# Compressed scores by stationaries of 32 key columns and four transposes; the two low-rank up projections alternate

## The reference

```
dist_c = t[:, None] - cmp_end[None, :]
lc = einsum('bghqd,bgcd->bghqc', qb, kc_blk) + shared_bias(dist_c)
pc = masked_softmax(lc, dist_c >= 0)
```

```
w_log = -softplus(-(w0 + tanh(wd) @ w_up)) - 0.5
a = sigmoid(a0 + ad @ a_up)
```

## Time and profile before

| | us |
|---|---|
| median of 3 runs | 652.71 (652.45 to 653.73) |
| the profiled execution's own time | 653.95 |
| its span, first to last instruction | 652.2 |
| TensorE matmul busy | 601.5 (92%) |
| TensorE weight load busy | 440.4 (68%) |
| VectorE busy | 218.5 (33%) |
| ScalarE busy | 138.3 (21%) |
| GpSimd busy | 20.6 (3%) |
| mean granted TensorE clock | 0.974 |
| DMA | 158.94 MB, mean 244 GB/s |

### The profile page before, as it was taken

How to read it: one execution, slowest core, us unless ns; L and a number is a source line. 1 busy time by engine, 2 the same in 40 slices (tenths; PEclk the granted TensorE clock), 3 DMA queues, 4 the chain that set the end, 5 groups by cost and what they waited for, 6 DMA issues and landing times.

```text
span 652.2 us, 11747 instructions
## 1 busy us (share of the span) xinstructions
PE 601.5 (92%) x4948; PEld 440.4 (68%) x4948; DVE 218.5 (33%) x599; ACT 138.3 (21%) x352; POOL 20.6 (3%) x24
## 2 busy tenths in 40 slices
PE   8999999999999999999999999998989988757684
PEld 8988887888877877777788888894344442313331
DVE  3152448634343666356410222235121111102022
ACT  3010233032234363343411000001210111000013
POOL 1000000000300003001000000000000000000000
PEclk9999999999999999999999999998999999959797
DMA  8585344731211111101329994887999999999992
GB/s 318 194 319 180 113 151 158 297 130 66 70 62 67 66 66 66 66 4 66 124 94 423 419 396 155 349 359 270 416 420 421 420 421 420 422 421 421 422 388 107
DMA packets 27287, 158.94 MB, mean 244 GB/s; under 512 B 2896, under 2 KB 7136, under 8 KB 9440
## 3 DMA queue, kind: packets, MB, share of 16 engines
q1 hardware_dynamic: 24224, 137.71, 54.0%
q10 hardware_dynamic: 3008, 20.45, 7.5%
HBM read 157.07 MB, written 1.07 MB: 243 GB/s over the span
## 4 chain that ended last, share of the span: by engine, by line
PE 61%; issue 32%; DVE 3%; DMA 2%; ACT 1%; SPq 0%; POOL 0%; POOLq 0%; DVEq 0%; ACTq 0%
PE bank L612 42%; PE bank L843 3%; PE bank L946 2%; PE bank L644 2%; PE bank L975 2%; DMA ring<-front 1%; PE bank L995 1%; PE bank L627 1%; PE bank L959 1%; ACT tok L1589 1%; PE bank L880 1%; PE bank L1011 1%; PE bank L899 1%; PE bank L910 1%; PE bank L1061 0%
## 5 line engine op out<-in xcount | busy, mean ns | idle before, releaser
L612 PE MATMUL bank<-hT,ring 128*128 128x256 f32 x864 | 199.7, 383 | 0.6 <-issue 0.3
L612 PEld LDWEIGHTS bank<-hT,ring 128*128 128x128 f32 x864 | 159.6, 190 | 30.7 <-issue 10.4
L612 PE MATMUL bank<-yT,ring 128*128 128x256 f32 x256 | 55.4, 379 | 0.0
L612 PEld LDWEIGHTS bank<-yT,ring 128*128 128x128 f32 x256 | 48.6, 190 | 6.6
L1423 ACT ACTIVATE work<-bank 128x512 f32<-128x512 f32 (+2 forms) x44 | 22.6, 514 | 107.5 <-PE bank L1242 48.9
L1788 DVE TENSOR_TENSOR work<-bank,table 128x512 f32<-128x512 f32 (+1 forms) x22 | 11.6, 544 | 95.9 <-PE bank L1235 88.1
L1288 PE MATMUL bank<-ring,work 128*32 128x512 f32 (+1 forms) x192 | 33.8, 634 | 10.2 <-DMA yT<-experts 7.1
L1235 PEld LDWEIGHTS bank<-work,tok 128*128 128x128 f32 x256 | 31.0, 196 | 10.4 <-issue 10.4
L1589 ACT ACTIVATE tok<-tok,small 128x128 f32<-128x128 f32 (+1 forms) x64 | 28.5, 445 | 23.2 <-DVE small L2015 21.6
L1235 PE MATMUL bank<-work,tok 128*128 128x128 f32 x256 | 32.5, 282 | 0.8 <-DVE work L1792 0.8
L1226 PE MATMUL bank<-ring,work 128*32 128x512 f32 x240 | 30.0, 606 | 2.3 <-DMA ring<-experts 2.3
(11 more groups left out here) (257 smaller groups left out, 742.6 us busy)
## 6 DMA issues: line engine op xcount, KB each, us to landing
ring<-front SPq DMA_DIRECT2D x47, 1024.0 KB, 5.0
ring<-experts SPq DMA_DIRECT2D x40, 1024.0 KB, 25.4
work<-experts SPq DMA_DIRECT2D x9, 1024.0 KB, 27.6
ring<-experts ACTq DMA_DIRECT2D x8, 1024.0 KB, 12.6
table<-experts SPq DMA_DIRECT2D x6, 1024.0 KB, 27.4
yT<-experts SPq DMA_DIRECT2D x6, 1024.0 KB, 26.8
hT<-experts SPq DMA_DIRECT2D x4, 1024.0 KB, 24.6
work<-experts ACTq DMA_DIRECT2D x3, 1024.0 KB, 27.9
```

The source lines that it names most:

```text
L612: return first(pe.matmul(o, l, r, start=(k == 0), stop=(k == n - 1)))
```

## The change

The scores. `kcb` is laid out as group, copy, key, with 16 places for the 15 keys, so that the 32 columns of one group (two copies of 16) are one stationary matrix. One memset of the whole replaces the two, and the two copies out of PSUM write with a stride. For each of the eight pairs of heads one matmul moves all 256 tokens; four pairs go into the four quarters of 32 partitions of one bank, in two column halves. The result has keys along the partitions, so ScalarE copies the bank `cs` into SBUF (`csT`), and after the step "turn" TensorE waits for that copy and transposes it by four transposes into bank 3. VectorE reads both tiles' scores from there.

The up projections. `wup` and `aup` are issued alternately, matmul by matmul, for n = 0 and then n = 1. The order of use of the banks and ScalarE's order are as before.

```diff
-        kcb = dead[:, at:at + 2 * NG * NCMP].rearrange("p (q n) -> p q n", q=2)
+        kcb = dead[:, at:at + NG * 32].rearrange("p (g q n) -> p g q n", g=NG, q=2)
+        csT = xf[:, 1024:1536].rearrange("p (b t) -> p b t", b=2)
...
-        hand("cs0", 2), hand("cs1", 3)
+        hand("cs", 2)
...
+            if name == "kw":
+                hand("csT", 3)
...
             for n in range(2):
-                o = begin(f"wup{n}")
+                up = [(f"wup{n}", 0, begin(f"wup{n}")), (f"aup{n}", 32, begin(f"aup{n}"))]
                 for m in range(2):
                     c = (2 * n + m) * P
-                    last = pe.matmul(o[:, m * S:(m + 1) * S], pr("lora_up")[0:32, c:c + P], mix[0:32, 12, :],
-                                     start=True, stop=True)
-                end(last, f"wup{n}")
-            for n in range(2):
-                o = begin(f"aup{n}")
...
+                    for name, row, o in up:
+                        last = pe.matmul(o[:, m * S:(m + 1) * S], pr("lora_up")[row:row + 32, c:c + P], mix[row:row + 32, 12, :],
+                                         start=True, stop=True)
+                        if m:
+                            end(last, name)
...
-            for i in range(NT):
-                nc_ = 7 if i == 0 else NCMP
-                o = begin(f"cs{i}")
-                for m in range(8):
-                    g = m // 2
-                    last = pe.matmul(o[:, 2 * m * nc_:2 * (m + 1) * nc_], qT[:, m, i * P:(i + 1) * P],
-                                     kcb[:, :, g * NCMP:g * NCMP + nc_], start=True, stop=True)
-                end(last, f"cs{i}")
+            o = begin("cs")
+            for b in range(2):
+                for m in range(4):
+                    last = pe.matmul(o[32 * m:32 * m + 32, b * S:(b + 1) * S], kcb[:, 2 * b + m // 2, :, :].rearrange("p q n -> p (q n)"),
+                                     qT[:, 4 * b + m, :], start=True, stop=True)
+            end(last, "cs")
 
             early(RWKV_STEPS[0])
             late(RWKV_STEPS[0])
+            pe.wait_ge(q["cmp_kv_ready"], 2)
+            turned("csT", [csT[:, b, i * P:(i + 1) * P] for i in range(NT) for b in range(2)])
             project("kw", C_KW)
...
-            act.wait_ge(q["keys_zeroed"], 2)
+            act.wait_ge(q["keys_zeroed"], 1)
             for p in range(2):
-                ins = copy(kcb[64 * p:64 * p + 64, p, :], b0[64 * p:64 * p + 64, 0:60])
+                ins = copy(kcb[64 * p:64 * p + 64, :, p, 0:NCMP],
+                           b0[64 * p:64 * p + 64, 0:NG * NCMP].rearrange("p (g n) -> p g n", g=NG))
             give(ins, "cmp_kv_ready", "kcb")
             keys(0, "ks")
+            b0 = full(act, "cs")
+            give(copy(csT, flat(b0)), "cmp_kv_ready", "cs")
...
-            for p in range(2):
-                chain(dve.memset(kcb[64 * (1 - p):64 * (1 - p) + 64, p, :], 0.0), "keys_zeroed", hold=False)
+            chain(dve.memset(kcb, 0.0), "keys_zeroed", hold=False)
...
-                b0 = full(dve, f"cs{i}")
+                b0 = full(dve, "csT")
...
-                chain(tt(cp, b0[:, 0:NH * nc_].rearrange("p (h n) -> p h n", h=NH), back, ALU.add))
-                dve.sem_inc(bank_free[plan[f"cs{i}"][0]], 1)
+                scored = b0[:, i * S:(i + 1) * S].rearrange("p (h n) -> p h n", h=NH)[:, :, 0:nc_]
+                chain(tt(cp, scored, back, ALU.add))
+                if i == NT - 1:
+                    dve.sem_inc(bank_free[plan["csT"][0]], 1)
```

## The result

The changed kernel takes 647.95 us (median of 4 runs, 647.42 to 648.79) against 652.97 us of the kernel before timed beside it: 5.0 us less, ratio 0.992, 95% interval 0.9901 to 0.9939. Forecast were 649.2 us with a range from 648.3 to 651.7. Timed once more the kernel had 648.4 us against 652.63, ratio 0.9931 (0.9912 to 0.9951), 4.2 us. Over all timed executions of the two kernels, 13 of this kernel and 62 of the kernel before, the medians are 648.2 and 653.0 us, 4.8 us apart.

The account below looks back on a forecast made before the run. TensorE's instruction stream bounds the kernel to about 440 us, the weights' arrival after 455 us. Savings of 0.55 + 3.0 = 3.5 us took the median from 652.71 to 649.2 us, range 648.3 to 651.7.

Parts of the forecast that it names:

- Part A: Up projections: alternating wup and aup makes two row groups run side by side, saving 0.55 us, between nothing and 1.0.
- The wait for bank 0: Before kc: ScalarE frees the bank only at 76.81, so kc starts at about 77.0 instead of 76.53.
- both waits for banks absent: Lower end of the range, 648.3 us: neither kc nor the first transposes wait for a bank's reader.
- Part B: Scores and transposes: scores in 1.15 us, twenty transposes at full clock, kw at 144.4 instead of 147.45, saving 3.0 us.
- the wait for bank 5: Before tok00: VectorE frees the bank after bonus1, so transposes start at 141.9 instead of 141.56, costing 0.35 us.
- The experts' stage: The stage bound by the weights' DMA, full share from 455 us: same length, 3.5 us earlier.
- The cover on VectorE: Softmax before the first mask: VectorE is done at 150.9, the mask is due at 152.6, leaving 1.7 us.
- What reaches the end: TensorE's saving counts in full: DMA share before 455 us is only 0.48, so the DMA-bound stretch begins earlier.
- 1: Rival: clock falls in the transposes or at kw's start, as long as before; 650.7 to 650.9 us, chance 0.14.
- 4: Rival: clock falls at the first transpose and stays down in kw; slower, up to 657.6 us, chance 0.04.
- (3): Rival: the scores' column quarters do not overlap, 651.8 us, or VectorE is late, similar end; chance together 0.06.
- (2): Rival: the gain does not reach the end, the last 200 us of weights not hanging on TensorE; 652.5 us, chance 0.06.

Follow-up runs that it names:

- the kernel with other banks: The kernel after with kc in bank 7, bonus1 in bank 1 and the first atok in bank 4: 648.26 us, ratio 0.9923 to the kernel before.

## Why the prediction was wrong

What it says of TensorE's own time, of the waits for banks and of the side-by-side work held, in place and in nearly every size. What failed is how it took the granted clock: it read the clock of one execution, and put the same clock into every execution, before and after.

- Part A, TensorE's own time: forecast 0.55, measured 0.61 in every profile that has the new order and the wait (2.28 us against 2.89). The wait for bank 0 was there (0.28), as forecast; taking it away saved 0.36.
- Part A, the clock: this is the first place where the step failed. The prediction counted the clock behind the up projections as 1.00 because it was 1.00 in the profile of before, and so gave the new order no gain from it and the low end of the range no room. In 2 of 6 profiles with the old order `kc` runs at 1.2 GHz, 1.7 us; with the new one in none of 10. On the mean that is 0.6 us, as much as part A's whole forecast, if the counts are the true chances. The range's lower end, "both waits for banks absent", should have had the 1.7 in it.
- Part B: forecast 3.0, measured 3.25 in the first pair of profiles: twenty transposes 0.115 each and not 0.125, and the wait for bank 5, 0.22 of idle time, was worth 0.34 when taken away, against 0.35. The scores with both changes of the tile size took 1.21 us from the `bonus` stream's end where no wait stood behind them (the kernel with other banks, 141.34 - 138.42 - 1.71), against 1.15. But the term is a mean of two cases: 3.25 where the old scores brought the clock down (3 of 5), 1.66 where they did not (7.16 against 5.50). The prediction had only the first case, as certain. The mean is 2.6, so here the error went the other way, 0.4 us too much.
- The experts' stage: the prediction put its change at nothing, "the same length". The clock at the gathering is a third draw, worth 1.3 to 1.5 us; it fell in 3 of 4 profiles of the kernel before and in 1 of 5 of the kernel after. If these were the true chances, it would be 0.8 us of gain; whether it is more than chance is open.
- The cover on VectorE: forecast 1.7 us left, 2.16 measured.
- What reaches the end: up to the gathering everything, as argued. From `kw` to the gathering it is even 0.2 us less: 300.46 to 300.48 us in five profiles with the old scores (in the sixth the half clock reached into `kw`), 300.26 to 300.35 in twelve with the new ones; and the full DMA share begins earlier. Behind the gathering's first 16 instructions the rest takes 199.5 to 201.1 us over all profiles, with either form of the two parts; a gain below 1 us, such as the 0.7 of the other banks, is lost in that.
- The fixed parts, those in every execution, are 0.61 + 1.66 + 0.2 = 2.5 us; the two places of the clock are worth 1.7 x 2/6 + 1.6 x 3/5 = 1.5 on the mean. That gives 4.0, near the second timing's 4.2 and 0.5 above the forecast's 3.5. What lifts the first timing to 5.0 and the gain over all executions to 4.8 is not shown. For the two profiled executions (6.4 us) the gathering's 1.3 us is seen in the traces; the first timing's other executions have no trace, and the two timings' intervals, 4.0 to 6.5 and 3.2 to 5.7 us, hold 4.0 as well.
- So the miss of 0.35 us below the range is in part luck: the second timing, 648.4 us of the same kernel, lies inside it. That the gain is above the forecast's 3.5 is not luck alone, since both timings and the 4.8 of all executions lie above it.
- Two slips in the sums changed nothing: the price of an old score instruction was read from the row's length (3.93/32), while their starts are 0.11 apart at full clock; and without the wait for bank 5 part B would save 3.4 and not 3.2, which is what the range's lower end used.
- Rivals: the clock stayed up in the transposes (1 and 4 fell), the quarters ran side by side (3), the gain reached the end (2).

The time is settled as far as the intervals go: 4.2 and 5.0 us lie in each other's interval. Not settled are what in the new scores saves the 0.2 us between `kw` and the gathering, whether the gathering's draw has changed, and why the clock falls in one execution and not in the next.

## What to carry to other kernels

A float32 matmul whose cost is its weight load is worth turning round, with the smaller operand as stationary, when the smaller stationary also lets several run side by side, and then even at the price of transposes afterwards: 3.65 us for 32 instructions at full clock became 1.07 for the scores and 0.5 for the transposes. The turning alone would have brought nothing here: sixteen instructions of 256 columns one after the other are 16 x 0.213 = 3.41 us, an estimate from the pace of `kw`.

Besides its own time, work that leaves most of the array empty for some microseconds (few moving columns, or one group of 32 rows) can go together with a fall of the clock in the dense work behind it, and it does so in some executions only. Look at the granted clock behind such a place in several profiles before giving it a price, and put the price times its frequency into the sum, and the full price into the range.

When two small matmuls use different rows or columns of the array they run side by side even some instructions apart in the program. The wait for a bank's reader is then the next thing in the way; taking it away shortened TensorE's stream by 0.7 us here and could not be seen in the time.

## What the runs showed of the hardware

- Transposes, also 52 in a row (5.7 us), kept the clock at 1.00; in a run of sixteen most of which lay at 0.50, it rose to 1.00 before the last had ended.
- The clock of 1.2 GHz hit the dense projection `kc` behind sixteen instructions of 32 rows (2.9 us) in 2 of 6 profiles and behind twice as many (6.6 us) in the one that tried it. Behind or within score matmuls of 14 and 30 columns it came in 3 of 5, with 112 and 120 columns, at the same pace of 0.11 us each, in none of one.
- TensorE overlaps instructions of different column quarters across four instructions of the same quarter: 1.09 against 1.07 us.
- A change from a stationary matrix of 128 columns to one of 32 cost 0.10 us (1.92 against 1.82 from `bonus` to the scores, new and old), and back about 0.15 (1.00 us from the first score to the first transpose in the kernel with other banks, less four rounds of 0.213 gives 0.15, an estimate).
